# Attention blocks issued in larger groups, and two kinds of follow-up copies moved within their iteration, in an eight-branch fp32 transformer kernel

## The reference, cut to what matters

```python
def one_block(qblk):                     # grouped-query: 8 query heads, 2 key heads, 4 blocks of 128 queries
    sc = jnp.einsum('blkgd,bskd->bkgls', qblk, k, preferred_element_type=F32) * scale
    p = jax.nn.softmax(sc, axis=-1).astype(v.dtype)
    return jnp.einsum('bkgls,bskd->blkgd', p, v)
...
    sc = jnp.einsum('blhmd,bshmd->bhmls', qblk, k, ...) * scale + bias[None, :, None]   # differential: 4 heads, 2 maps each
    p = jax.nn.softmax(sc, axis=-1)
    w = (p[:, :, 0] - lam * p[:, :, 1]).astype(v.dtype)
    return jnp.einsum('bhls,bshd->blhd', w, v)
```

## Time and profile before

| | |
|---|---|
| median of three runs | 3388.97 us |
| the profiled execution, its own time | 3389.38 us |
| its span in the profile | 3388.1 us |
| TensorE matmul busy | 98% |
| weight load / VectorE / ScalarE / GpSimd busy | 75% / 45% / 41% / 43% |
| share of the ending chain on TensorE | 91% |

### The profile page before, as it was taken

How to read it: one execution, slowest core, us unless ns; L and a number is a source line. 1 busy time by engine, 2 the same in 40 slices (tenths; PEclk the granted TensorE clock), 3 DMA queues, 4 the chain that set the end, 5 groups by cost and what they waited for, 6 DMA issues and landing times.

```text
span 3388.1 us, 39090 instructions
## 1 busy us (share of the span) xinstructions
PE 3305.3 (98%) x14246; PEld 2535.8 (75%) x14246; DVE 1512.7 (45%) x2792; ACT 1394.2 (41%) x2610; POOL 1455.8 (43%) x1116
## 2 busy tenths in 40 slices
PE   8999999999999999999999999998999999899999
PEld 6667776878888667776688888764788886478887
DVE  5544666344534544466544455556322235632222
ACT  3543445343323344344534333456433335643322
POOL 3234442445554323443345555440455544135544
PEclk9999999999999999999999999999999999999999
DMA  4122221233322212222223333210233222023333
GB/s 142 63 80 73 72 66 60 91 107 108 100 97 92 64 57 68 69 69 66 65 91 117 114 98 97 90 57 13 89 109 97 97 90 69 19 71 109 97 97 100
DMA packets 155078, 281.96 MB, mean 83 GB/s; under 512 B 19172, under 2 KB 20965, under 8 KB 154886
## 3 DMA queue, kind: packets, MB, share of 16 engines
q1 hardware_dynamic: 154598, 279.39, 25.9%
q10 hardware_dynamic: 288, 0.07, 0.0%
HBM read 276.62 MB, written 2.77 MB: 82 GB/s over the span
## 4 chain that ended last, share of the span: by engine, by line
PE 91%; DVE 4%; ACT 3%; DMA 1%; issue 1%; SPq 1%; POOL 0%; ACTq 0%; DVEq 0%; POOLq 0%
PE bank L547 26%; PE bank L549 26%; PE bank L548 26%; PE bank L605 3%; PE bank L614 2%; PE bank L778 1%; PE bank L790 1%; PE bank L579 1%; PE bank L920 1%; PE bank L735 1%; PE bank L657 1%; PE bank L846 1%; PE bank L912 0%; DMA raw<-in_units 0%; ACT work L1003 0%
## 5 line engine op out<-in xcount | busy, mean ns | idle before, releaser
L2127 POOL TENSOR_TENSOR wl<-raw,wh 128x512 fp32r<-128x512 f32 x1012 | 1380.5, 1371 | 1916.8 <-ACT wh L989 1880.8
L547 PE MATMUL bank<-Uh,wh 128*128 128x512 f32 x2720 | 1116.9, 411 | 9.8 <-DVE Ul L1444 7.4
L549 PE MATMUL bank<-Uh,wl 128*128 128x512 f32 x2720 | 1066.8, 392 | 0.0
L548 PE MATMUL bank<-Ul,wh 128*128 128x512 f32 x2720 | 1064.6, 391 | 0.0
L989 ACT ACTIVATE wh<-raw 128x512 fp32r<-128x512 f32 x1012 | 625.0, 626 | 1065.9 <-PE bank L549 1040.5
L547 PEld LDWEIGHTS bank<-Uh,wh 128*128 128x128 f32 x2720 | 514.1, 189 | 160.1 <-issue 43.2
L548 PEld LDWEIGHTS bank<-Ul,wh 128*128 128x128 f32 x2720 | 514.5, 189 | 118.5 <-issue 14.4
L549 PEld LDWEIGHTS bank<-Uh,wl 128*128 128x128 f32 x2720 | 513.3, 189 | 111.0
L1433 DVE TENSOR_TENSOR work<-bank,rs 128x512 f32<-128x512 f32 x308 | 212.5, 690 | 768.6 <-PE bank L549 728.2
L547 PE MATMUL bank<-Hh,wh 128*128 128x512 f32 x1258 | 504.7, 401 | 4.4 <-DVE small L1708 1.9
L549 PE MATMUL bank<-Hh,wl 128*128 128x512 f32 x1258 | 490.4, 390 | 0.0
(11 more groups left out here) (235 smaller groups left out, 2739.5 us busy)
## 6 DMA issues: line engine op xcount, KB each, us to landing
raw<-in_units SPq DMA_DIRECT2D x1012, 256.0 KB, 2.7
xT<-in_xT SPq DMA_DIRECT2D x8, 256.0 KB, 4.8
out<-xT SPq DMA_DIRECT2D x8, 256.0 KB, 2.6
table<-scratch SPq DMA_DIRECT2D x16, 112.0 KB, 3.1
work<-in_dft SPq DMA_DIRECT2D x2, 512.0 KB
work<-in_counts SPq DMA_DIRECT2D x2, 512.0 KB, 5.2
table<-scratch SPq DMA_DIRECT2D x48, 16.0 KB, 2.6
const<-in_const SPq DMA_DIRECT2D x1, 576.0 KB, 7.7
```

The source lines that it names most:

```text
L547: nc.tensor.matmul(out, H, xh, start=k == 0, stop=False)
L548: nc.tensor.matmul(out, H, xl, start=False, stop=False)
L549: mm = nc.tensor.matmul(out, L, xh, start=False, stop=k == x.kt - 1)
L2127: nc.gpsimd.tensor_tensor(g.wl[:, a:a + PK * P], g.raw[:, a:a + PK * P], g.wh[:, a:a + PK * P].bitcast(F32), ALU.subtract).then_inc(g.s_lo, 1)
```

## The change

Grouped-query stage: four tasks in an iteration instead of two. All four scores are issued together, into banks 2 to 5; after them come four rounds of one `turn_over` and four k-steps each. All turned tiles go through bank 6. Chains q1, q2 and q3 use bank 7, which the values use too. Differential stage: two tasks in an iteration. Their four score matmuls are issued together with one `turn_over`; then six k-steps, the other `turn_over`, six k-steps. VectorE and ScalarE follow the same order. Layers 3 and 4: VectorE runs `turned` and `values` at the end of iteration t instead of after `maximum(t+1)`.

```diff
-        return Chain(name, src, tmp, normed, ..., "mean64", (3, 2, 6, 5)[t], "rot64", cos, sin,
+        return Chain(name, src, tmp, normed, ..., "mean64", (3, 7, 7, 7)[t], "rot64", cos, sin,
...
-ATTN = {"gqa": ((2, 3, 4), (5, 6)), "diff": ((2, 3, 4, 5), (6,)), "pairs": ((2, 3), (5, 6))}
+ATTN = {"gqa": ((2, 3, 4, 5), (6,)), "diff": ((2, 3, 4, 5), (6,)), "pairs": ((2, 3), (5, 6))}
...
# TensorE, grouped-query
-        for x in range(n + 3):          # n = 16
+        for x in range(n + 2):          # n = 8
...
-                for hd in range(2):
-                    scores(i, "gqa", tasks, 2 * x + hd)
+                for t in range(4 * x, 4 * x + 4):
+                    scores(i, "gqa", tasks, t)
+            for r in range(4 if x <= n else 2):
+                if 0 <= x - 1 < n:
+                    turn_over(i, "gqa", tasks, 4 * x - 4 + r, probs[r])
+                if (x, r) == (0, 1):
+                    turn_rope(i, chains["q1"])
+                if x in (2, 4) and r == 0:
+                    mean(i, chains[f"q{1 + x // 2}"])
+                if x in (2, 4) and r == 3:
+                    turn_rope(i, chains[f"q{1 + x // 2}"])
+                if x >= 3 and x % 2 and r == 0:
...
+                advance(4)
+                beat(i, "gqa", x, r)
# TensorE, differential
-        for t in range(n + 6):          # n = 16
+        for x in range(n // 2 + 3):
+            if x < n // 2:
+                pe.wait_ge(s_dve, at("V", "ev", i, "dk", tasks[2 * x].head))
+                for t in (2 * x, 2 * x + 1):
+                    scores(i, "diff", tasks, t)
+            if 0 <= x - 1 < n // 2:
+                turn_over(i, "diff", tasks, 2 * x - 2, probs[(2 * x - 2) % 3])
...
+            if x in (2, 5):
+                h = 2 if x == 2 else 3
+                finish_of(i, "dv", h)
+                turn_values(i, f"d{h}", w(16), 7, (s_dve, at("V", "ev", i, "dv", h)))
+            else:
+                advance(6)
+            beat(i, "diff", x, 0)
+            if 0 <= x - 1 < n // 2:
+                turn_over(i, "diff", tasks, 2 * x - 1, probs[(2 * x - 1) % 3])
+            advance(6)
+            beat(i, "diff", x, 1)
# ScalarE, grouped-query
+            for r in range(4 if x <= n else 2):
+                if x < n:
+                    soften(i, "gqa", tasks, 4 * x + r, probs)
+                if 0 <= x - 1 < n:
+                    keep_turned(i, "gqa", tasks, 4 * x - 4 + r)
+                if x in (2, 4) and r == 0:
+                    name = f"q{1 + x // 2}"
+                    rstd(i, name, g.gqa_chain(i, name).bank, g.gqa_chain(i, name).tmp)
...
# VectorE, layers 3 and 4
                 maximum(i, "pairs", tasks, t, None)
             if t - 1 in MEANS:
                 after_mean(MEANS[t - 1])
-            if t - 1 in TURNS:
-                turned(i, g.chain_of(i, TURNS[t - 1]))
-            if t - 1 in VALUES:
-                values(i, f"l{VALUES[t - 1]}", 7, g.pair_tiles(VALUES[t - 1])[2])
             if 0 <= t - 2 < n:
                 normalise(i, "pairs", tasks, t - 2, None)
             beat(i, "pairs", t)
...
+            if t in TURNS:
+                turned(i, g.chain_of(i, TURNS[t]))
+            if t in VALUES:
+                values(i, f"l{VALUES[t]}", 7, g.pair_tiles(VALUES[t])[2])
```

More of the change, by code:

```diff
@@ L331, in gqa_chain @@
         src, normed, tmp = ((m(4), m(6), m(7)), (m(5), m(0), m(2)), (w(12), w(14), w(16)), (w(13), w(15), w(27)))[t]
[L332 removed]
+        return Chain(name, src, tmp, normed, self.small[:, 40:41], "mean64", (3, 7, 7, 7)[t], "rot64", cos, sin,
                      self.gqa_q(t), tmp)
@@ L713, in layer1 @@
         tasks = g.gqa_tasks()
-        n = len(tasks) // 2
+        n = len(tasks) // 4
         probs = [w(4 + r) for r in range(4)]
-        for x in range(n + 3):
+        for x in range(n + 2):
             if x < n:
@@ L719, in layer1 @@
                     pe.wait_ge(s_dve, at("V", "rope", i, "k"))
-                if x % 4 == 0:
-                    pe.wait_ge(s_dve, at("V", "rope", i, f"q{x // 4}"))
-                for hd in range(2):
-                    scores(i, "gqa", tasks, 2 * x + hd)
[L724 to L748, removed]
+                if x % 2 == 0:
+                    pe.wait_ge(s_dve, at("V", "rope", i, f"q{x // 2}"))
+                for t in range(4 * x, 4 * x + 4):
+                    scores(i, "gqa", tasks, t)
@@ new lines, in layer1 @@
+            for r in range(4 if x <= n else 2):
[8 more added lines that the diff above has]
+                if x >= 3 and x % 2 and r == 0:
+                    pair = tasks[4 * x - 6:4 * x - 4]
+                    pe.wait_ge(s_act, at("C", "pT", i, "gqa", 4 * x - 5))
+                    pe.wait_ge(s_dve, at("V", "vt", i, "gqa"))
+                    take(7, s_dve, "V", "H", i, 1, pair[0].head // 2)
+                    for m in range(NT):
+                        for hd, k in enumerate(pair):
+                            mm = nc.tensor.matmul(bank[7][hd * HQ:(hd + 1) * HQ, :],
+                                                  w(24)[:, m * P + hd * HQ:m * P + (hd + 1) * HQ],
+                                                  k.probT[:, m * S:(m + 1) * S], start=m == 0, stop=m == NT - 1)
+                            if m == NT - 1:
+                                mm.then_inc(s_pe, T("pv", i, "gqa", k.head))
+                advance(4)
+                beat(i, "gqa", x, r)
@@ L822, in layer1 @@
         probs = [w(r) for r in range(3)]
-        for t in range(n + 6):
[L824 to L834, removed]
-                output_mean(i, 3)
[L836 to L841, removed]
+        for x in range(n // 2 + 3):
[5 more added lines that the diff above has]
+                turn_over(i, "diff", tasks, 2 * x - 2, probs[(2 * x - 2) % 3])
+            if x == 1:
+                output_mean(i, 3)
+            if x >= 3 and x % 2:
+                k = tasks[2 * x - 3]
+                pe.wait_ge(s_act, at("C", "pT", i, "diff", 2 * x - 3))
                 pe.wait_ge(s_dve, at("V", "vt", i, f"d{k.head}"))
@@ L1227, in layer1 @@
         beat(i, "F", 14)
-        rstd(i, "q1", 2, g.gqa_chain(i, "q1").tmp)
+        rstd(i, "q1", 7, g.gqa_chain(i, "q1").tmp)
         beat(i, "F", 15)
         tasks = g.gqa_tasks()
-        n = len(tasks) // 2
+        n = len(tasks) // 4
         probs = [[w(4 + r) for r in range(4)]]
[L1234 to L1247, removed]
-            beat(i, "gqa", x, 0)
-            beat(i, "gqa", x, 1)
+        for x in range(n + 2):
+            for r in range(4 if x <= n else 2):
[6 more added lines that the diff above has]
+                    rstd(i, name, g.gqa_chain(i, name).bank, g.gqa_chain(i, name).tmp)
+                if x >= 3 and x % 2 and r == 0:
+                    head = tasks[4 * x - 5].head
+                    act.wait_ge(s_pe, at("T", "pv", i, "gqa", head))
+                    branch_high(i, 1, head // 2, bank[7][:, :])
+                beat(i, "gqa", x, r)
             if x == n - 1:
```

103 lines of the change are left out of this document (54 added, 49 removed).

## The result

| | before | after |
|---|---|---|
| median | 3388.55 us | 3360.13 us |
| lowest and highest | 3387.36, 3389.11 | 3357.36, 3360.19 |
| span of the profiled execution | 3388.1 us | 3358.9 us |

The ratio is 0.9915, with a 95% interval of 0.9903 to 0.9928, so the change is worth 28.4 us; the sum of the prediction had 19.6. The direction and the stated range (3356 to 3382) hold; the narrower range that I gave the forecast itself (3363 to 3377) does not. The sum is 9 us short.

What follows compares the result with a forecast made beforehand. TensorE, its matmuls busy 98% of the span, bounds the kernel. 2 x (-2.9 - 3.8 - 3.6 + 1.0) + 2 x (-0.5) = -19.6 us takes 3389.4 to 3369.8, stated as 3370; range 3356 to 3382.

Steps and rivals of the forecast that it cites:

- Scores in one run: Layers 1 and 2: four scores in a run cost 2.11 us instead of 2.54; grouped-query stage -2.9 us a layer.
- rival that runs gain nothing: Score runs in layers 1 and 2: each pair pays its 0.43 us again, 13.8 less gained, 3384; chance 0.09.
- Waits of the grouped-query stage: Layers 1 and 2: 5.6 us of bank waits go, 2.0 charged for late copies; net -3.6 us a layer.
- Differential stage: Layers 1 and 2: eight pairs of tasks give -3.8 us, new waits cost +1.0, a layer.
- the wait I left in place: Start of the differential stage: the 2.0 us wait for bank 2 stays, as the same copy frees it.
- Layers 3 and 4: VectorE's moved turned and values: losses at t = 24, gains at t = 38 and 40; -0.5 us a layer.
- fourth rival: Layers 3 and 4 lose: full slow stretch after t = 24, gain at t = 40 taken again; +4.2 a layer, 3379; chance 0.13.
- third rival: Layers 3 and 4: all copy waits and slow stretches go, 13.5 us a layer, 3344; half of it 3357; chance 0.10 together.
- One bank for all turned tiles: Grouped-query stage, a rival: ScalarE's copies come late and TensorE waits 64 times, up to +45 us, 3415; chance 0.08.
- a slow stretch at t = 24: Layers 3 and 4: half clock may follow the grown 3.8 us wait; taken as +1.5 us, bounds 0 and +2.6.

Runs made afterwards that it cites:

- e3: The changed kernel with one k-step put between the two pairs of each group of four scores, grouped-query and differential stages; 3369.62 us.
- e2: The kernel before with only chain q1 of the grouped-query stage moved from bank 2 to bank 7; 3375.99 us, ratio 0.9966.
- e10: The kernel before with the differential part of the change alone; 3382.00 us, ratio 0.9976.
- e11: The kernel of e6 with the transposed values of differential head 1 in bank 6 instead of bank 2; 3344.22 us.
- e1: The changed kernel with VectorE's turned and values in layers 3 and 4 back behind maximum(t+1); 3358.62 us.
- e8: The changed kernel with grouped-query rounds of two and six k-steps in turn instead of four and four; 3378.19 us.
- e5: The changed kernel run again, unedited, for a second trace and set of times; 3359.74 us.
- e6: The changed kernel with ScalarE's exp moved behind the evictions, rstd and pooled high part at six places in layers 3 and 4; 3349.48 us.

## Why the prediction came out as it did

- **Scores in one run**: right. 2.12 us for four against 2.11 in the forecast; -2.7 against -2.9 in the grouped-query stage. e3 shows the 0.43 us from the other side. The rival that runs gain nothing falls.
- **Waits of the grouped-query stage**: this is the term that was mis-sized most. "I charge 2.0 us a layer" measured 0. My layout put the copy beside q2's mean 0.9 us late; it is 0.05 us early. I had the operations right, but took their order in time too loosely, and I should have written it row by row as in the fence above.
- **The clock behind q1's wait**: a term missing from the sum. The stretch at half clock from 112 to 116 us stands in the trace of before, 1.6 us a layer, and I looked at the clock only in layers 3 and 4. e2 (4.1 us a layer for 2.2 of wait) and the other traces without the wait show that it goes with the wait, e10 that it is not there in every execution.
- **Differential stage**: -3.05 a layer against -2.8, with the waits at +0.8 against +1.0; e11 adds that the wait I left in place was worth removing.
- **Layers 3 and 4**: the forecast of -0.5 a layer was nearer than the pair of traces. My terms were +3.6 at t = 24 and -4.1 at t = 38 and 40; the means over eight to twelve stretches are +3.2 and -4.5, and +0.2 between. Of the +3.2, 1.7 stand without half clock (forecast 2.1) and 1.5 come with it (forecast 1.5). By e1 the whole move can't be told from nothing in the time. The fourth rival (a loss there) and the third (all 13.5 us a layer) both fall.
- **The range**: that it held is in part luck. The bounds of my own terms ended at 3363, and 3360.1 lies below. The range reached to 3356 only for the sake of half the third rival, whose mechanism fell; the two terms that missed both lay in layers 1 and 2, where no rival stood on the fast side.
- **One bank for all turned tiles**: it did not decide at four k-steps, and e8 shows where it would. The Trainium skill ("TensorEngine Tiling (Array Packing)", "PSUM Bottleneck") warns that copies out of PSUM may become the bottleneck. e8's wait of 1.80 us for line 1176 is such a bound, at two k-steps.

In sum, a layer of the first kind: 2.0 for waits that did not come, 1.6 of clock, 0.25 in the differential stage, less 0.2 in the score runs and less 0.5 that I can't place, and 0.6 for a layer of the second kind. That is 3.75, twice it 7.5, and with the 19.6 of the forecast 27.1 of the 28.4 us measured. The remaining 1.3 is inside the interval (24 to 33 us). The 1.6 of clock counts in full here, as in the trace of before; e10 shows an execution of that stage without it, so how much of it is in the median is open. The part that stays open is what makes a stretch at half clock come or not behind the same wait; no run here was made for that.

## What to carry to other kernels

Short waits of a busy TensorE cost more than their length in some executions, so a shared bank that makes it wait 2 us is worth changing even where a sum by the wait alone looks small. Before reading a difference of a few microseconds from two traces, look at a stage that the edit does not touch and take the same stage from several kernels that share it: here that turned 2.4 us a layer into 1.1. Where an in-order engine gets a step moved, look at the order of its partner too: moving VectorE's step gave 1.1 us a layer by the stretches (in the time it can't be told from nothing), and 5 more once ScalarE's exp was moved to fit it, while the second move without the first lost.

## What the hardware showed that I had not expected

- Behind one and the same wait the granted clock falls in one execution and not in the next: 2.19 us at line 585 (before with 0.63 us records, e10 with 0.39), 2.04 us at line 605 (2.71 us for the scores in e5, 1.99 in e6). At these two places in layers 1 and 2 a fall costs 1.6 us; at t = 15 to 24 of layers 3 and 4 it cost up to 2.9 (47.0 against 44.1).
- Even a wait of 3.56 us isn't always followed by a fall. TensorE at t = 24 of layer 3 in e3, where after had 3.22 us for the same values, and of layer 4 in after itself:

```profile
2289.77 1.71 PE L916 MATMUL bank<-work 128*64 128x128 f32 x14 [3.56 <-DVE small L1715]
...
2881.85 1.71 PE L912 MATMUL bank<-work 128*64 128x128 f32 x14 [3.56 <-DVE small L1711]
```

  The Trainium skill ("TensorE: Matmul & The Clock Gate", "What's actually happening") has the throttled state as the default, which made me call a slow stretch at t = 24 certain by that rule; these two rows disagree, and layer 3 of after agrees.
- A wait as long as 2.74 us at t = 38 left the clock at 1.00 in after, while one of 2.19 us did not in before. The same 3.41 us at line 579 left it full in layer 3 of e1 and not in before. So the length of the wait alone does not tell.
- A run of score matmuls on half the array's rows costs some 0.43 us once, beside 0.42 for each matmul: 1.27 us for two, 2.12 for four.
